# Two reorders: low halves of weights by VectorE outside the first attention; modulation groups under the norms' roots and the first scan keys ahead of x's norm

## The chip, the cores and the metric
One core of one Trainium2 chip runs the whole program. The metric is device microseconds of one execution. A core has five engines that work side by side: TensorE (PE, with its weight loads shown as PEld), VectorE (DVE), ScalarE (ACT), GpSimd (POOL) and SyncE (SP, which here only issues DMAs). Each walks its own instruction list in order and meets the others through semaphores.

## The reference
Two different transformer blocks, each of depth 2, work on 256 tokens of width 1024. Cut to what matters here:

```
def first_block(x, ...):                      # l = 0, 1
    h = rms_norm(x, ln_attn_g[i])             # "a0", "a1"
    ... = split(h @ w_in[i]); y_diff, y_moba = two kinds of causal attention
    x = x + concat([y_diff, y_moba]) @ w_out[i]
    x = x + conv_ffn(rms_norm(x, ln_ffn_g[i]), w_up[i], ..., w_down[i])   # "f0", "f1"

def second_block(x, c, ctx, c_ctx, ...):      # l = 0, 1
    mod_l = silu(c) @ w_ada[l] + b_ada[l]     # shift, scale, gate: 3 x 1024
    mod_c = silu(c_ctx) @ w_ada[l] + b_ada[l]
    h_l = _rmsnorm(x,  g_pre[l]) * (1 + sc_l) + sh_l     # "x0", "x1"
    h_c = _rmsnorm(xc, g_pre[l]) * (1 + sc_c) + sh_c     # "c0", "c1"
    pl, pc = h_l @ w_in[l], h_c @ w_in[l]     # attention, gated linear scan, convolution, gates
    out = (g_a*br_a + g_b*br_b + g_c*br_c) @ w_out[l]
    x = x + gt_l * _rmsnorm(out_l, g_post[l])
```

All arrays are float32.

## The kernel before
**Products.** Each float32 product is made of three matmuls on split numbers: high half by high half, low by high, high by low. Activations and weights are both split. A weight tile of 128 x 1024 (512 KB) is loaded by SyncE (L2552) into one of NR = 5 `RAW` buffers; ScalarE copies its high half to `SPH` (L1335); VectorE (L1873) or GpSimd (L2450) subtracts and writes the low half `SPL`, both into one of NS = 4 slots. TensorE's helper `turned` runs the triples L888 to L890 (weights stationary), `straight` runs L900 to L902 (activations stationary). A `RAW` buffer is free after the low half, a slot after its last matmul.

**One order.** The class `Schedule` is run once to write a single list of steps (loads, splits, products, norms, copies); each engine's program walks that list and emits its own share, so the list fixes the order on every in-order queue, SP's loads among them. `get_w` names the next tile and lets splits run NS + 1 tiles ahead; a load stands in the list NR - 1 tiles ahead of its split. Which engine makes a low half follows a pattern over the split tiles:

```
SPLIT_ON = ((0, 0, 1), (1, 1, 1))
eng = "pool" if self.split_on[self.nsplit % len(self.split_on)] else "dve"
```

The first entry holds outside the first block's attention (every third low half on GpSimd), the second inside it (all on GpSimd, while VectorE does the softmaxes). At the start, and in a few tiles between the two depths of the second block, all are on VectorE; in `group_n` with `by_tile`, the PF = 2 tiles ahead are on GpSimd. The low halves of odd activation tiles of the three branches (`ABL`, L2496) are GpSimd's too.

**The norms.** `norm` adds the step `stats` (VectorE and ScalarE sum the squares, L1935 and L1357, then VectorE takes the root in a chain of small operations L1809 to L1819 and builds diagonal matrices `DG`, L1943) and eight steps `prod`, four matmuls each: TensorE multiplies x by the diagonals (L934), which turns it, and ScalarE and VectorE or GpSimd write the split result `HTH` (L1365, or L1374 and L1377) and `HTL` (L1951, or L2473). For a1, f0, f1 and x0 nothing stands between the last use of the old x and the norm in TensorE's order.

**The modulation.** `ada_te` makes `mod` of depth 0 in six groups of 512 columns of `w_ada`: four steps of eight matmuls straight from `RAW` (L946, no split), a copy of the row by ScalarE (L1341), and eight small matmuls that turn it (L955), then an add on VectorE (L1878). Two groups run in the first attention (`fill`), four in the first feed-forward layer, one step in each of its 24 rounds j:

```
if l == 0:
    next(self.ada, None)
```

After the sixth group VectorE makes `GP`, the scale for c0 and x0 (L1883). c0's products run in the second attention.

**The scan's keys.** After x0's norm come `rank` (24 matmuls with a 32 column weight, L1057 to L1059) and four tiles `gk` of `wgk0`, each 24 matmuls of 512 columns: 256 of context (from c0, ready long before) and 256 of x (from x0). The rest of the second block follows: query projections, the gated linear scan (L2163, L2169, L1111), the branches, attention, gates and the output product.

## Time and profile before

| | before |
|---|---|
| three runs | 2269.45, 2271.2 and 2271.24 us, median 2271.2 |
| the profiled execution's own time | 2270.02 us |
| its span | 2267.9 us |
| TensorE busy, mean granted clock | 2131.5 us (94%), 0.967 |
| VectorE, ScalarE, GpSimd busy | 1326.3, 963.0, 556.8 us |
| low halves on GpSimd, on VectorE | 169, 293 |

The span runs from the first to the last instruction that the profile shows; the execution's own time has another 2.1 us around it. A granted clock of 1 is TensorE's full 2.4 GHz and 0.5 is 1.2 GHz; a mean over a stretch lies between. The text below names the view of each number it uses.

### The profile page before, as it was taken

The page shows a single profiled execution, that of the slowest core. Times are in us where ns is not written, and L with a number is a line of the kernel's source. Part 1 is how long each engine was busy: PE and PEld are TensorE (multiplying, and loading weights), DVE is VectorE, ACT ScalarE, POOL GpSimd, SP SyncE. Part 2 cuts the span into 40 slices and gives each one's busy share as a digit, 9 for nine tenths or more (in the row PEclk, how much of TensorE's full clock was granted, in tenths as well). Part 3 has the DMA queues.
Part 4 walks back from the last instruction along what each step waited for, and adds up shares of the span by engine and source line. Part 5 has one row for each costly group of instructions (what it writes and reads, how often), then busy time and mean ns, then how long its engine had stood idle before and what let it go on. Part 6 is the DMA issues. An engine that isn't in the chain of part 4 may idle for free.

```text
span 2267.9 us, 31387 instructions
## 1 busy us (share of the span) xinstructions
PE 2131.5 (94%) x12074; PEld 1825.8 (81%) x12074; DVE 1326.3 (58%) x2202; ACT 963.0 (42%) x1602; POOL 556.8 (25%) x321
## 2 busy tenths in 40 slices
PE   7888999889899899998999999999999998999998
PEld 5667998667899787887887778888778898888987
DVE  5735666774777513827464453877464577575464
ACT  4434555444455425334332363233343553445443
POOL 1422333152333311111031002222222121321332
PEclk9979999898999999999999999999999999999999
DMA  9434655331455422211132202634224233241543
GB/s 251 132 130 153 242 212 210 127 114 53 146 186 179 154 101 82 67 57 65 57 103 84 75 19 88 226 125 148 95 95 151 93 112 131 89 162 66 172 147 128
DMA packets 79066, 285.00 MB, mean 126 GB/s; under 512 B 8822, under 2 KB 9730, under 8 KB 78920
## 3 DMA queue, kind: packets, MB, share of 16 engines
q1 hardware_dynamic: 70560, 256.15, 33.3%
q10 hardware_dynamic: 6072, 18.73, 2.3%
q0 software_dynamic: 2288, 8.13, 1.4%
q8 instruction: 97, 1.59, 0.3%
q14 instruction: 49, 0.40, 0.1%
HBM read 277.14 MB, written 5.83 MB: 125 GB/s over the span
## 4 chain that ended last, share of the span: by engine, by line
PE 42%; DVE 7%; ACT 3%; issue 2%; POOL 0%; POOLq 0%; DVEq 0%; ACTq 0%
PE pb L888 8%; PE pb L890 8%; PE pb L889 8%; PE pb L900 3%; PE pb L902 3%; PE pb L901 3%; PE pb L1214 2%; PE pb L906 2%; ACT SPH L1335 1%; PE pb L1195 1%; DVE SPL L1873 1%; PE pb L1111 1%; PE pb L1155 1%; DVE GW L2163 1%; DVE ATT L2191 1%
## 5 line engine op out<-in xcount | busy, mean ns | idle before, releaser
L2450 POOL TENSOR_TENSOR SPL<-RAW,SPH 128x1024 fp32r<-128x1024 f32 x169 | 415.8, 2463 | 1058.9 <-ACT SPH L1335 960.1
L1873 DVE TENSOR_TENSOR SPL<-RAW,SPH 128x1024 fp32r<-128x1024 f32 (+1 forms) x293 | 426.5, 1463 | 415.6 <-ACT SPH L1335 386.3
L888 PE MATMUL pb<-HTH,SPH 128*128 128x256 f32 (+1 forms) x1984 | 648.6, 327 | 5.4 <-POOL HTL L2473 2.0
L889 PE MATMUL pb<-HTL,SPH 128*128 128x256 f32 (+1 forms) x1984 | 638.1, 322 | 0.0
L890 PE MATMUL pb<-HTH,SPL 128*128 128x256 f32 (+1 forms) x1984 | 637.8, 321 | 0.0
L1335 ACT ACTIVATE SPH<-RAW 128x1024 fp32r<-128x1024 f32 x462 | 476.5, 1048 | 278.3 <-PE pb L902 117.6
L888 PEld LDWEIGHTS pb<-HTH,SPH 128*128 128x128 f32 x1984 | 382.8, 193 | 39.1 <-issue 6.7
L889 PEld LDWEIGHTS pb<-HTL,SPH 128*128 128x128 f32 x1984 | 383.0, 193 | 27.0
L890 PEld LDWEIGHTS pb<-HTH,SPL 128*128 128x128 f32 x1984 | 382.4, 193 | 27.0
L900 PE MATMUL pb<-SPH,HTH 128*128 128x512 f32 x544 | 221.3, 407 | 19.6 <-DVE SPL L1873 9.0
L901 PE MATMUL pb<-SPH,HTL 128*128 128x512 f32 x544 | 216.4, 398 | 0.0
L902 PE MATMUL pb<-SPL,HTH 128*128 128x512 f32 x544 | 216.3, 398 | 0.0
L900 PEld LDWEIGHTS pb<-SPH,HTH 128*128 128x128 f32 x544 | 105.0, 193 | 47.5 <-issue 11.6
L888 PE MATMUL pb<-ABH,SPH 128*128 128x512 f32 (+1 forms) x384 | 132.0, 344 | 10.4 <-POOL ABL L2496 7.6
L890 PE MATMUL pb<-ABH,SPL 128*128 128x512 f32 (+1 forms) x384 | 130.2, 339 | 0.0
L889 PE MATMUL pb<-ABL,SPH 128*128 128x512 f32 (+1 forms) x384 | 130.1, 339 | 0.0
L902 PEld LDWEIGHTS pb<-SPL,HTH 128*128 128x128 f32 x544 | 104.8, 193 | 23.0
L901 PEld LDWEIGHTS pb<-SPH,HTL 128*128 128x128 f32 x544 | 105.3, 193 | 20.8
L888 PEld LDWEIGHTS pb<-ABH,SPH 128*128 128x128 f32 x384 | 72.5, 189 | 19.5 <-ACT ABH L1746 8.0
L2483 POOL TENSOR_TENSOR AL<-FT,AH 128x256 fp32r<-128x256 f32 x44 | 32.6, 741 | 210.6 <-ACT AH L1466 210.6
L1696 ACT ACTIVATE GT<-pb,BG 128x512 f32<-128x512 f32 (+1 forms) x48 | 27.8, 579 | 127.7 <-PE pb L890 127.7
L890 PEld LDWEIGHTS pb<-ABH,SPL 128*128 128x128 f32 x384 | 72.5, 189 | 8.6
(275 smaller groups left out, 2947.6 us busy)
## 6 DMA issues: line engine op xcount, KB each, us to landing
RAW<-in_w_up SPq DMA_DIRECT2D x88, 512.0 KB, 4.3
RAW<-in_wa SPq DMA_DIRECT2D x64, 512.0 KB, 3.2
RAW<-in_w_in SPq DMA_DIRECT2D x48, 512.0 KB, 4.6
RAW<-in_wmg SPq DMA_DIRECT2D x48, 512.0 KB, 3.3
RAW<-in_wbr SPq DMA_DIRECT2D x48, 512.0 KB, 3.2
RAW<-in_w_down SPq DMA_DIRECT2D x44, 512.0 KB, 3.4
RAW<-in_w_ada SPq DMA_DIRECT2D x24, 512.0 KB, 5.0
ARAW<-in_w_ada ACTq DMA_DIRECT2D x24, 512.0 KB, 4.1
```

The lines of the kernel that those rows point to most:

```text
L888: T.matmul(o, wh[:, kt, :], xh[:, kt, n0:n1], start=kt == 0, stop=False)
L889: T.matmul(o, wh[:, kt, :], xl[:, kt, n0:n1], start=False, stop=False)
L890: m = T.matmul(o, wl[:, kt, :], xh[:, kt, n0:n1], start=False, stop=kt == 7)
L900: T.matmul(P[:, :], xh[:, kt, c], wh[:, j, :], start=kt == 0, stop=False)
L901: T.matmul(P[:, :], xl[:, kt, c], wh[:, j, :], start=False, stop=False)
L902: m = T.matmul(P[:, :], xh[:, kt, c], wl[:, j, :], start=False, stop=kt == 7)
L906: return T.transpose(o, i, ident)
L1214: m = T.matmul(P[:, t * 128:(t + 1) * 128], sb["VV"][:, k0 + i, (h // 4) * 128:(h // 4 + 1) * 128], sb["APT"][:, j % 2, i * 128:(i + 1) * ...
L1335: A.activation(hi, raw, ACT.Copy, scale=1.0).then_inc(*act.tick(s["hi"], ("u", u)))
L1873: W.tensor_tensor(lo, raw, hi.bitcast(F32), SUB).then_inc(*dve.tick(s["lo_dve"], ("u", u)))
L2450: G.tensor_tensor(lo, raw, hi.bitcast(F32), SUB).then_inc(*pool.tick(s["lo_pool"], ("u", u)))
L2483: G.tensor_tensor(sb["AL"][:, i, :], sb["FT"][:, j % 2, :], sb["AH"][:, i, :].bitcast(F32), SUB).then_inc(*pool.tick(s["ffn_pool"], ("al", ...
```

## The change
Three things, in the order list alone and in what follows from it:

- **Low halves.** `SPLIT_ON[0]` becomes `(0,)`: outside the first block's attention every weight's low half is VectorE's. `low_by_pool` names the activation tiles whose low half stays with GpSimd: odd ones of branch a, and of branches b and c at depth 0; at depth 1 those of b and c move to VectorE. In the last group of `w_out`, splits run 6 tiles ahead and not 2.
- **Modulation groups.** A new `norm_filled` puts one group between `stats` and the products of a norm: one under f0 (bank 7), one under a1 (bank 3), one under f1 (bank 7); one stays in the first feed-forward layer, one step in each round j from 1 to 6; two stay in the first attention. `limit` holds back how far splits may run ahead during this. `GP` is made after the fourth group, and `gate_col` waits for the last two.
- **Keys.** The context half (columns 256 to 511) of the first EARLY = 3 key tiles is multiplied ahead of x0's products, which share banks 0 to 6 with the three accumulations that are held; the x half follows the norm, then `rank`, then the fourth tile.

```diff
--- before.py
+++ after.py
@@ -33,12 +33,13 @@
 RA = [2.0, 1.25]
 IC, PC = (4, 5), (8, 15)
 KEYS = ((0,) * 8, (3, 3, 1, 2, 2, 2, 2, 1))
+EARLY = 3
 BO = (4, 4, 4)
 RB = (2, 2, 2.8, 4)
 OUTS = (4, 2, 5)
 RQ = ((.8, .7, 2), (.8, 1, 3))
 GA = [2, 1]
-SPLIT_ON = ((0, 0, 1), (1, 1, 1))
+SPLIT_ON = ((0,), (1,))
 PF = 2
 LT, LV = 2, 3
 
...
@@ -115,6 +116,11 @@
         drain(side)
 
 
+def low_by_pool(l, w, kt):
+
+    return kt % 2 == 1 and (w == "a" or w in "bc" and l == 0)
+
+
 def gla_full(s, l):
 
     return s == 0 or l == 0
...
@@ -189,7 +194,7 @@
         self.gets += 1
         if self.order is not None:
             assert self.order[u] == (name, idx, cols, kind)
-            self.split_upto(u + NS + 1)
+            self.split_upto(min(u + NS + 1, self.limit))
         return u
 
     def put_w(self, u):
...
@@ -213,9 +218,7 @@
                     for u in us:
                         self.put_w(u)
                     if ahead:
-                        self.split_on[:] = (1,)
                         self.split_upto(self.gets - 1 + ahead)
-                        self.split_on[:] = SPLIT_ON[0]
                 yield t
             return
         for i in range(4):
...
@@ -232,6 +235,21 @@
         for _ in self.products(tag, ring):
             next(side, None)
         drain(side)
+
+    def norm_filled(self, tag, ada_ring):
+
+        self.add("stats", tag)
+        self.ada_ring = ada_ring
+        self.limit = self.gets + 4
+        for n, _ in enumerate(self.fill(1)):
+            if n == 4:
+                self.limit += 1
+                self.split_upto(self.limit)
+        for kt, _ in enumerate(self.products(tag, LOW7)):
+            if kt in (1, 4):
+                self.limit += 1
+                self.split_upto(self.limit)
+        self.limit = 1 << 30
 
     def products(self, tag, ring):
         for kt in range(8):
...
@@ -349,7 +367,10 @@
         self.add("bias_back")
 
     def block1(self, l):
-        self.norm(f"a{l}", LOW7, () if l else self.first(), 1)
+        if l:
+            self.norm_filled("a1", (3,))
+        else:
+            self.norm("a0", LOW7, self.first(), 1)
         self.add("lam", l)
         if l:
             self.add("mark", f"qkv{l}")
...
@@ -383,11 +404,12 @@
         drain(first)
         for g in range(2):
             if g:
-                drain(self.group_n(("wo", l, 1), f"w_out{l}", 1, (0, 1), (2, 3), ("Y", l), True))
+                drain(self.group_n(("wo", l, 1), f"w_out{l}", 1, (0, 1), (2, 3), ("Y", l), True, 4 + PF))
             for t in range(2):
                 self.add("res1", l, g, t)
                 self.give(("wo", l, g, t))
-        self.norm(f"f{l}", LOW7)
+        self.norm_filled(f"f{l}", (7,))
+        self.ada_ring = (3,)
         for t in range(2):
             for g in range(2):
                 self.take((4 + 2 * t + g,), ("dn", l, t, g))
...
@@ -401,8 +423,8 @@
                     self.put_w(u)
                 self.add("up", l, j)
                 self.give(n)
-            if l == 0:
-                next(self.ada, None)
+            if l == 0 and 1 <= j < 7:
+                next(self.ada)
             if j == 3 and l == 0:
                 self.add("tables", 0)
             if j == 6 and l == 0:
...
@@ -650,20 +672,35 @@
         if not last:
             self.add("mark", "x1done")
         self.add("wdec", l)
+        early = []
         if not last:
+            self.limit = self.gets + EARLY - 1
+            for ft in range(EARLY):
+                self.take((0, 1, 2, 3), ("gk", l, ft))
+                early.append(self.get_w(f"wgk{l}", ft))
+                self.add("gk_mm", l, ft, early[ft], 1)
             self.norm("x0", LOW7)
             self.add("spill_x")
+            self.limit = 1 << 30
+            self.split_upto(self.gets)
         self.add("mark", f"proj{l}")
+        for ft, u in enumerate(early):
+            self.add("gk_mm", l, ft, u, 0)
+            self.put_w(u)
+            self.split_upto(self.gets + ft + 1)
+            self.add("gk", l, ft)
+            self.give(("gk", l, ft))
         u = self.get_w(f"wr{l}", 0, cols=256)
         n = self.take(ALL8, ("wr", l))
         self.add("rank", l, u, H)
         self.put_w(u)
         self.give(n)
-        for ft in range(4):
+        for ft in range(len(early), 4):
             u = self.get_w(f"wgk{l}", ft)
             n = self.take(ALL8, ("gk", l, ft))
-            self.add("gk", l, ft, u, H)
+            self.add("gk_mm", l, ft, u, None)
             self.put_w(u)
+            self.add("gk", l, ft)
             self.give(n)
         if not last:
             drain(self.gla_queries(0, H))
...
@@ -718,12 +755,10 @@
                     self.give(("w2", l, 0, t))
         if not last:
             self.add("stats", "x1")
-            self.split_on[:] = (0,)
             for t in (2, 3):
                 self.split_upto(self.gets + t - 2)
                 self.x_out(l, t)
             self.split_upto(self.gets + 2)
-            self.split_on[:] = SPLIT_ON[0]
             drain(self.products("x1", LOW6))
             for ft, _ in enumerate(self.gla_queries(1, ("x1",))):
                 if ft == 0:
...
@@ -873,7 +908,7 @@
         if src[0] == "AB":
             _, l, w = src
             pe.wait_ge(s["branch_act"], ("h", l, w, kt))
-            pe.wait_ge(s["branch_pool" if kt % 2 and w != "s" else "branch_dve"], ("l", l, w, kt))
+            pe.wait_ge(s["branch_pool" if low_by_pool(l, w, kt) else "branch_dve"], ("l", l, w, kt))
             return ABH, ABL
         for tag in src:
             pe.wait_ge(s["norm_act"], ("h", tag, kt))
...
@@ -1059,10 +1094,18 @@
             m = T.matmul(P[0:32, :], wl[:, kt, :], xh[:, kt, :], start=False, stop=kt == 7)
         m.then_inc(*pe.tick(mm, ("w", u), ("wr", l)))
 
-    def gk(l, ft, u, src):
-        P = bank(("gk", l, ft))
-        m = turned(P[:, :], *halves(u), src, 0, 512)
-        m.then_inc(*pe.tick(mm, ("w", u), ("gk", l, ft)))
+    def gk_mm(l, ft, u, st):
+
+        src = ("x1", "c1") if l else ("x0", "c0")
+        if st != 0:
+            bank(("gk", l, ft))
+        P = k.P(("gk", l, ft))
+        if st is None:
+            m = turned(P[:, :], *halves(u), src, 0, 512)
+        else:
+            m = turned(P[:, st * 256:st * 256 + 256], *halves(u), src[st:st + 1], st * 256, st * 256 + 256)
+        if not st:
+            m.then_inc(*pe.tick(mm, ("w", u), ("gk", l, ft)))
 
     def gq(l, ft, u, src):
         n = 256 if l else 512
...
@@ -1877,8 +1920,8 @@
         dve.wait_ge(mm, ("ada", g))
         W.tensor_tensor(MT[:, 0, 4 * g:4 * g + 4, :], P[:, 256:264].rearrange("p (j s) -> p j s", j=4),
                         V(par("b_ada", 4 * g, 4), [1, 4], [0, 2]), ADD).then_inc(*dve.free(*k.read(("ada", g))))
-        if g == 5:
-            for i in range(6):
+        if g == 3:
+            for i in range(4):
                 dve.wait_ge(*k.read(("ada", i)))
             W.scalar_tensor_tensor(out=sb["GP"][:, 0, :, :], in0=MT[:, 0, 8:16, :], scalar=1.0,
                                    in1=V(par("g_pre", 0, 8), [1, 8], [0, 2]), op0=ADD, op1=MUL).then_inc(
...
@@ -2354,12 +2397,14 @@
                                op0=MUL, op1=MUL).then_inc(*dve.free(*k.read(("og", l, ft))))
 
     def split_z(l, w, ft):
-        if ft % 2 == 0:
-            split_low(l, w, ft, sb["ZB"][:, 0, 0:256 if l else 512])
+        if not low_by_pool(l, w, ft):
+            split_low(l, w, ft, sb["ZB"][:, ft % 2, 0:256 if l else 512])
 
     def gate_col(l):
         k.past(dve, f"rows{l}")
         dve.wait_ge(s["const_dve"], ("mod", l))
+        for g in () if l else (4, 5):
+            dve.wait_ge(*k.read(("ada", g)))
         for st in range(1 if l else 2):
             W.tensor_tensor(sb["GC"][:, st, :], MT[:, l, 16:24, st], par("g_post", l * 8, 8), MUL).then_inc(
                 *dve.tick(s["branch_dve"], ("gc", l, st)))
...
```

## Rows read from the trace of the kernel before

**Rows 1.** The profile page: engines' busy time, costliest groups, weight loads.
```profile
PE 2131.5 (94%) x12074; PEld 1825.8 (81%) x12074; DVE 1326.3 (58%) x2202; ACT 963.0 (42%) x1602; POOL 556.8 (25%) x321
...
L2450 POOL TENSOR_TENSOR SPL<-RAW,SPH 128x1024 fp32r<-128x1024 f32 x169 | 415.8, 2463 | 1058.9 <-ACT SPH L1335 960.1
L1873 DVE TENSOR_TENSOR SPL<-RAW,SPH 128x1024 fp32r<-128x1024 f32 (+1 forms) x293 | 426.5, 1463 | 415.6 <-ACT SPH L1335 386.3
...
RAW<-in_w_up SPq DMA_DIRECT2D x88, 512.0 KB, 4.3
```

**Rows 2.** Waits of TensorE: releaser, us in total, times, longest.
```profile
PE pb L934 <- DVE DG L1943: 27.2, 5, 7.9
PE pb L1111 <- DVE GW L2169: 11.1, 8, 3.4
...
PE pb L900 <- DVE SPL L1873: 9.0, 5, 3.4
PE pb L888 <- POOL ABL L2496: 7.6, 2, 4.2
```

**Rows 3.** Windows: stretch, length, PE, PEld, DVE, ACT, POOL busy, clock, DMA, GB/s.
```profile
181.65:192.70 11.05, 5.33 (x34) 5.20 (x33) 7.62 (x22) 2.93 (x7) 2.09 (x1) 0.69 0.29 95
...
770.85:785.30 14.45, 6.55 (x34) 6.43 (x33) 6.93 (x20) 6.12 (x13) 3.12 (x5) 0.65 0.26 83
...
1842.00:1912.00 70.00, 60.74 (x476) 59.88 (x475) 58.64 (x78) 25.28 (x33) 12.04 (x5) 0.95 0.34 114
2023.80:2034.00 10.20, 7.04 (x35) 6.23 (x34) 6.46 (x6) 2.10 (x4) 1.76 (x1) 0.67 0.50 183
```

**Rows 4.** Windows, the same columns: the two feed-forward stretches.
```profile
192.70:396.85 204.15, 203.80 (x1483) 183.24 (x1481) 133.16 (x185) 108.44 (x161) 69.29 (x44) 1.00 0.61 217
578.30:770.85 192.55, 189.42 (x1323) 176.27 (x1321) 141.10 (x191) 103.71 (x157) 73.05 (x44) 1.00 0.53 176
```

**Rows 5.** Timeline around norm f0: start, us, engine, operation, idle before.
```profile
182.63 2.19 DVE L1935 SCALAR_TENSOR_TENSOR XN<-XS 128x1024 f32<-128x1024 f32 x1
...
187.53 5.40 PE L934 MATMUL pb<-DG,XS 128*128 128x128 f32 x32 [5.72 <-DVE DG L1943]
```

**Rows 6.** Timeline, TensorE: norm products of a1 and x0, then c1's.
```profile
403.76 6.46 PE L934 MATMUL pb<-DG,XS 128*128 128x128 f32 x32 [6.75 <-DVE DG L1943]
...
778.90 6.62 PE L934 MATMUL pb<-DG,XS 128*128 128x128 f32 x32 [7.90 <-DVE DG L1943]
...
1705.73 0.28 PE L890 MATMUL pb<-HTH,SPL 128*128 128x256 f32 x1
...
1706.81 0.28 PE L890 MATMUL pb<-HTH,SPL 128*128 128x256 f32 x1
1707.10 4.11 PE L934 MATMUL pb<-DG,XS 128*128 128x128 f32 x32
```

**Rows 7.** Timeline, TensorE: one modulation step in the first feed-forward stretch.
```profile
359.05 0.64 PE L946 MATMUL pb<-RAW,CSP 128*32 128x256 f32 x8
```

**Rows 8.** Timeline after x0's norm: rank, a low half of x0, first keys.
```profile
785.27 0.48 PE L1057 MATMUL pb<-HTH,SPH 128*32 128x512 f32 x1
...
787.94 0.74 POOL L2473 TENSOR_TENSOR HTL<-HV,HTH 128x256 fp32r<-128x256 f32 x1 [0.17 <-ACT HTH L1377]
...
789.06 1.22 DVE L1873 TENSOR_TENSOR SPL<-RAW,SPH 128x1024 fp32r<-128x1024 f32 x1 [10.11 <-ACT SPH L1335]
...
790.88 0.39 PE L888 MATMUL pb<-HTH,SPH 128*128 128x512 f32 x1
```

**Rows 9.** Low halves on GpSimd in the second attention: us, busy (count), clock, DMA.
```profile
443.00:550.00 107.00, 34.72 (x15) 0.87 0.27 89
```

**Rows 10.** Timeline of one collision of GpSimd and VectorE, late in the kernel.
```profile
2023.16 2.40 POOL L2450 TENSOR_TENSOR SPL<-RAW,SPH 128x1024 fp32r<-128x1024 f32 x1 [6.51 <-ACT SPH L1335]
...
2023.37 2.73 DVE L2296 TENSOR_TENSOR QNB<-QNB,QT 128x512 f32<-128x512 f32 x1
...
2026.25 0.41 PE L906 MATMUL pb<-IDENT,QNB 128*128 128x128 f32 x2 [1.84 <-DVE QNB L2296]
```

More of the change, by code:

```diff
@@ L132, in __init__ @@
         self.slots, self.raw_before, self.slot_before = [None] * NS, {}, {}
-        self.split_on = [0]
-        self.low_at = {}
+        self.split_on, self.limit = [0], 1 << 30
         self.run()
@@ L1241, in tensor_program @@
             "bias": bias, "qk_turn": qk_turn, "scores": scores, "turn": turn1, "values": values, "y_turn": y_turn,
-            "up_mm": up_mm, "down": down, "rank": rank, "gk": gk, "gq": gq, "gdec": gdec,
+            "up_mm": up_mm, "down": down, "rank": rank, "gk_mm": gk_mm, "gq": gq, "gdec": gdec,
             "gprod": gprod, "gke": gke, "gst": gst, "gout": gout, "ba_mm": ba_mm, "head_turn": head_turn,
@@ L1509, in rank, with gk @@
             *act.free(*k.read(("wr", l))))
-    def gk(l, ft, u, src):
+    def gk(l, ft):
         act.wait_ge(mm, ("gk", l, ft))
@@ L1735, in z @@
             act.wait_ge(s["branch_act"], ("h", l, w, ft - 2))
-            act.wait_ge(s["branch_pool" if ft % 2 else "branch_dve"], ("l", l, w, ft - 2))
+            act.wait_ge(s["branch_pool" if low_by_pool(l, w, ft) else "branch_dve"], ("l", l, w, ft - 2))
         A.activation(sb["ZB"][:, ft % 2, 0:NT], k.P(("z", l, w, ft))[:, 0:NT], ACT.Tanh, scale=0.5).then_inc(
@@ L2504, in split_z @@
     def split_z(l, w, ft):
-        if ft % 2:
+        if low_by_pool(l, w, ft):
             split_low(l, w, ft, sb["ZB"][:, 1, 0:256 if l else 512])
```

## The prediction

> **What bounds the kernel now.** The page first: TensorE is busy 2131.5 of 2267.9 us [rows 1], so at most 136 us of waiting and what a reduced clock costs can be won without taking matmuls away. VectorE is busy 1326 us, GpSimd 557. Then TensorE's waits: the largest entry is the norm's, 27.2 us in five waits on the diagonals `DG` [rows 2]; behind it come waits on VectorE's scan operation L2169, on low halves of weights and, twice, up to 4.2 us, on GpSimd's `ABL`. Then the windows round the norms: in f0's 11.05 us TensorE works 5.33, at a mean granted clock of 0.69; x0's is 14.45 us at 0.65 [rows 3]. The timelines show one shape at f0, a1, f1 (which repeats f0) and x0: TensorE idle for 5.7, 6.75, 5.7 and 7.9 us, then 32 norm products that last 5.40, 6.46 and 6.62 us where c1's, which follow close matmuls, last 4.11 [rows 5, 6]. So TensorE idles, its clock goes towards the 1.2 GHz level, and the next products pay too. Last, pairs of GpSimd and VectorE: a low half of 2.40 us begins at 2023.16, VectorE's L2296 begins 0.21 later and lasts 2.73 us, up to 2026.10, and TensorE waits 1.84 for it [rows 10]. 2.73 is what was left of the 2.40, 2.19, and a remainder of 0.54. The 10 us behind it have clock 0.67 [rows 3].
>
> **Part 1, three modulation groups put under the roots of f0, a1 and f1.** A group in the feed-forward stretch costs its TensorE time. The first such stretch has four groups and the second none: 204.15 against 192.55 us, busy 203.80 against 189.42 [rows 4]: 2.9 us a group by span, 3.6 by busy time. By the operations, four steps of 0.64 [rows 7] and one turn of about 0.9: 3.5. I take 3.4 (bounds 2.9 and 3.6), so 10.2 us leave the two feed-forward and attention paths. In the norm the group costs nothing if it fits the gap. At half clock its steps double to about 1.14 us each, some 5.5 with the turn, and ScalarE's copy of the row adds about 0.8 between them: 6.3 against gaps of 5.7 to 6.75. That is tight, but the first steps run before the clock falls, and the activity itself keeps it up. VectorE's chain of the root has only the small add of the group behind it. The move past SP's queue: the four raw tiles fill four of five `RAW` buffers, so the first `w_up` or `w_in` tiles are issued only when TensorE has finished modulation steps; each lands 3 to 4.3 us later [rows 1], then ScalarE's high half (1.05) and VectorE's low half (1.22 [rows 8]) follow, between the norm's own writes. The 32 products cover 4 to 5 us of this. I book +1.7 for what isn't covered, over three norms (0 to +6). Part 1: -10.2 + 1.7.
>
> **The squares' sum.** At f0 and f1 VectorE's L1935 lasts 2.19 us because a GpSimd low half is running [rows 5]; alone such an operation on 128 x 1024 takes 1.22, by the low half with as many elements [rows 8]. With those low halves on VectorE, behind `stats` in its queue, -0.95 at each: -1.9 (0 to -2).
>
> **Clock in the norms.** With matmuls in the gap the norm's products would last 4.11 and not 5.40 (f0, f1) and 6.46 (a1) [rows 5, 6]: 1.3 + 1.3 + 2.35 = 5.0. The first steps of a group are few columns and may not hold the clock, and ScalarE's and VectorE's copies pace the products: I take a third, -1.6 (0 to -5).
>
> **Part 2, early keys.** A tile's context half is 24 matmuls of 256 columns at 0.12 us (nine pitches from 1705.73 to 1706.81 [rows 6]): 2.88 us, 8.6 for three. They start where TensorE now stops, at 770.9, and end at 779.5, 0.6 after the diagonals are ready at 778.90 [rows 6]. The products then run at the full clock. What ends the norm is the chain behind them: ScalarE takes about 0.95 us per 256 columns of two copies, and the last low half of x0 is done at 788.68 [rows 8]. Before, `rank` covers that; after, the first key tile's x half does, and is done at about 789.05. Then two x halves (5.76), `rank` (785.27 to 790.88: 5.61 [rows 8]), and the fourth tile (5.45): 805.9, against 790.88 + 4 x 5.45 = 812.7. That is -6.8; I take -6.5 (bounds -5, if a weight is late, and -8, if ScalarE starts on the early products' heels).
>
> **Part 3, low halves to VectorE.** GpSimd has 169 low halves of about 2.4 us, of which two times 15, in the attentions, stay (one of these shown [rows 9]): 139 move. Each adds 1.22 us to VectorE alone, and takes GpSimd's reads off it. How often VectorE pays for these now: its 293 own low halves average 1.463 against 1.22 alone, +71 us in this line alone [rows 1, 8], and L1935 and L2296 show that other lines pay too [rows 5, 10]. Added work: 139 x 1.22 = 170. So VectorE's sum rises by something between 0 and 100 us of its 1326, which no one waits for in itself. On TensorE's path I find nine waits that end behind such a pair, 20 us together (the longest 4.2 and, for L2169, 3.4 [rows 2]; 1.84 [rows 10]); of these the collision itself is some 1.4 us each, 12.5. Queueing behind low halves that are now VectorE's gives back 4. The clock behind these waits (10.2 us at 0.67 [rows 3] and three like it) gives back 4, and new waits in dense stretches cost 4. Part 3: -12.5 + 4 - 4 + 4 = -8.5 (bounds +4 and -20).
> The Trainium skill, page "SBUF — State Buffer", section "Who interferes with whom", says that a VectorE instruction with two SBUF inputs contends with a GpSimd instruction that reads SBUF, and that the later one is blocked until the other ends. By that rule, the trace agrees: 2.73 us is the rest of the GpSimd one and most of its own. Taken at its word every moved low half frees VectorE entirely, and part 3 would tend to its -20 end.
>
> **The sum.** -10.2 + 1.7 - 1.9 - 1.6 - 6.5 - 8.5 = -27.0. On the profiled execution's own 2270.0 us (2.1 round its span) that gives 2243.0; the runs' median of 2271.2 stands 1.2 above the profiled one, so 2244.
>
> **The rivals.** (a) VectorE's low halves cost as much as GpSimd's did: part 3 is 0, the rest stands: -18, 2253. For it: VectorE gains net work, and TensorE already waits 9.0 us in five waits on its low halves [rows 2]. Chance 0.20. (b) The norms keep most of their gaps because the tiles behind a modulation group come late: a group hides in TensorE's wait, but 3 us of new wait follow at each of three norms, and part 3 gives half: 2271.2 - 27 + 9 + 4 = 2257. For it: the `RAW` buffers. Against: 3.2 to 4.3 us of landing lie under 5 us of products. Chance 0.08. (c) More: all collision waits and their clock go, and the norms' products run at full clock: 10.2 + 1.9 + 5 + 7 + 12 = 36, 2235. For it the rows of c1. Chance 0.12. (d) Nothing comes of it: the groups in the feed-forward stretch were hidden and the norms' gaps are refilled by waits: 2271. Against: busy 203.80 of 204.15 hides nothing [rows 4]. Chance 0.02. (e) The other side: VectorE's in-order queue becomes the bound. In the scan stretch of depth 1 it is busy 58.64 of 70 us, 84% [rows 3], with 12.04 of GpSimd's beside it. Each moved low half that stands before a scan or softmax operation that TensorE waits for costs 1.2 us there, and gains nothing. Against gains of 18 it decides once more than 15 of the 139 do so, and with 24 the kernel is at 2271 - 18 + 29 = 2282. Against it: most of the 139 lie in stretches where VectorE is busy 65 to 73% [rows 4] and its operation ahead of a low half would have been slowed. Chance 0.03.
> The Trainium skill, page "Perfetto Trace Analysis", section "Optimizing Scalar/DVE Operations", says that work of a saturated DVE may be better on Scalar or GPSIMD, though a shared read port can spoil it. That speaks against this change in the 84% stretch, where it would give (e); the trace bears out the half about the port more than the half about saturation.
>
> **How the numbers follow.** The forecast has 0.55. The bounds of single terms lie far apart (part 3: 24 us), so the range goes from rival (c) with 2 us to spare, 2233, to above (b), 2261; it leaves out (d), (e) and half a tail on either side. A difference under 0.2%, 4.5 us, is about what a measurement of this kernel can't tell from no change. Faster than that: all but (d) and (e) and a remainder, 0.94; same 0.03; slower 0.03.
>
> **What the profile of the changed kernel would show.** Right: TensorE's waits on `DG` fall from 27.2 us to under 8; the first feed-forward stretch is about 8 to 11 us shorter, the second unchanged; x0's keys end 6 to 7 us sooner after the last feed-forward matmul; norm windows have a clock above 0.8; L1873 x432 with a mean near 1.25 us and L2450 x30; waits on `ABL` L2496 at depth 1 gone, L2296 at 0.69 throughout. Wrong: new waits of L888 and L900 on `SPH` or `SPL` directly behind the norm's products (rival b); waits on GW, ATT or QNB that end behind an L1873 (rivals a, e); clock near 0.6 in the norms although TensorE is active.

## The result and the profile after

The changed kernel takes 2211.8 us (median of 4 runs, 2210.3 to 2217.8) against 2270.4 for the kernel before (2269.5 to 2271.2): ratio 0.9747, 95% interval 0.9727 to 0.9766, or some 58 us. The forecast was 2244, with a range down to 2233. The direction was right; the size was not, and the time is below the range.

The profiled execution has a span of 2211.3 us (own time 2213.1) against 2267.9, so 56.6 us have to be found. The page, in the lines that answer to [rows 1]:

```profile
PE 2112.7 (96%) x12146; PEld 1816.3 (82%) x12146; DVE 1361.5 (62%) x2350; ACT 961.3 (43%) x1602; POOL 206.2 (9%) x173
...
L1916 DVE TENSOR_TENSOR SPL<-RAW,SPH 128x1024 fp32r<-128x1024 f32 x433 | 524.2, 1229 | 412.9 <-ACT SPH L1378 397.4
...
L2495 POOL TENSOR_TENSOR SPL<-RAW,SPH 128x1024 fp32r<-128x1024 f32 x29 | 69.3, 2402 | 186.2 <-ACT SPH L1378 137.7
...
RAW<-in_w_up SPq DMA_DIRECT2D x88, 512.0 KB, 4.5
```

TensorE is busy 96% of a shorter span, and for 18.8 us less, although it has 72 more matmuls. Most of that is the clock (mean granted 0.977, before 0.967): it was busy at the 1.2 GHz level for 117.6 us before and is for 84.6 now, and half of the difference, 16.5 us, is what the lower level costs. L1916 is L1873 of before: 433 low halves with a mean of 1.229 us, where 293 had 1.463. So 140 more low halves cost VectorE 524.2 - 426.5 = 98 us in this line, and its whole busy time rose by only 35 us (1326.3 to 1361.5): the rest it got back in other lines. GpSimd's own fell from 169 to 29 (the prediction had 139 moved and 30 left).

TensorE's waits, beside [rows 2] (us in total, times, longest):

```profile
PE pb L935 <- DVE SPL L1916: 6.3, 3, 3.4
PE pb L969 <- DVE DG L1986: 6.2, 4, 2.6
...
PE pb L1154 <- DVE GW L2212: 4.5, 8, 1.4
PE pb L923 <- DVE ABL L2291: 4.3, 2, 2.9
```

The wait for the norms' diagonals went from 27.2 to 6.2 us, GpSimd's `ABL` has left the list of waits at depth 1 (VectorE's `ABL` L2291 has 4.3), L2169's successor L2212 went from 11.1 to 4.5, and the waits on VectorE's low halves, which rival (e) expected to grow, fell from 9.0 in five to 6.3 in three.

The windows that answer to [rows 3]: norm f0, x0's norm with the early keys, the scan of depth 1, and the first 8 us behind the former collision:

```profile
181.95:192.23 10.28, 8.44 (x73) 7.18 (x72) 8.44 (x24) 6.50 (x11) 0.00 (x0) 0.83 0.80 306
745.40:758.60 13.20, 12.69 (x104) 12.26 (x104) 6.53 (x20) 4.86 (x11) 2.17 (x3) 1.00 0.36 124
1806.10:1869.40 63.30, 59.41 (x489) 58.54 (x488) 56.36 (x80) 24.41 (x33) 0.00 (x0) 1.00 0.38 119
1979.50:1987.50 8.00, 6.18 (x45) 5.21 (x43) 4.83 (x7) 2.63 (x6) 0.00 (x0) 1.00 0.74 251
```

Clock 0.83 for 0.69 in f0, 1.00 for 0.65 in x0's norm, 1.00 for 0.95 in the scan and 1.00 for 0.67 behind the collision. The scan's window is a little wider than that of before: the same matmuls took 70.1 us before and take 61.8 now. The two feed-forward stretches, beside [rows 4]:

```profile
192.23:384.20 191.97, 191.97 (x1361) 178.01 (x1360) 133.59 (x202) 102.75 (x156) 16.35 (x22) 1.00 0.57 196
557.42:745.30 187.88, 187.87 (x1321) 176.33 (x1321) 136.98 (x213) 103.72 (x157) 16.45 (x22) 1.00 0.54 178
```

The first went from 204.15 to 191.97 us, the second from 192.55 to 187.88, although no modulation group was ever in it.

To see where the 56.6 us arise, the same matmul was looked up in both traces, and the difference of its start times taken. Plotted over time it is a stair: flat where both kernels are equally fast, a step where one gains. Its treads were read at these places (times of before):

| up to | stretch | this stretch gives |
|---|---|---|
| 187.5 | start, first attention, wait of f0 | -0.7 |
| 394.0 | f0's products, first feed-forward layer | -11.9 |
| 411.2 | norm a1 | -0.8 |
| 447.5 | projections of the second attention | -6.6 |
| 573.1 | second attention, wait of f1 | -1.0 |
| 768.0 | second feed-forward layer | -4.3 |
| 807.2 | x0's norm and keys | -6.8 |
| 1233.0 | scan of depth 0 | -5.0 |
| 1844.3 | branches to output, depth 0 | +1.2 |
| end | depth 1 of the second block | -20.7 |

The first feed-forward layer and x0's norm with its keys account for 18.7 of it. The other 38 lie elsewhere, over half of them in the last fifth of the kernel, which only the low halves touch. Single treads are good to a few us only: the start differs by 1 to 3 us between executions, and two steps of +1.2 and +1.5 us behind 1270 and 1630 stand in this trace and in e2's, but not in e4's or e5's.

The f0 norm after, on TensorE, beside [rows 5]:

```profile
182.01 1.93 PE L981 MATMUL pb<-RAW,CSP 128*32 128x256 f32 x32
184.44 1.05 PE L990 MATMUL pb<-SEL,AROW 128*128 128x2 f32 x8 [0.50 <-ACT AROW L1384]
186.84 5.44 PE L969 MATMUL pb<-DG,XS 128*128 128x128 f32 x32 [1.34 <-DVE DG L1986]
192.23 0.39 PE L923 MATMUL pb<-HTH,SPH 128*128 128x256 f32 x1
```

The 32 modulation matmuls and the 8 that turn the row are in what was an idle gap of 5.72 us, with 0.5 us of waiting for ScalarE's copy between them; the norm's products start at 186.84, earlier than the 187.53 of before, and the first product of the feed-forward layer follows them at once. The group takes 3.5 us here, up to 185.49, where the prediction had 6.3. So the group is free. The norm's products are no faster: 5.44 us against 5.40.

x0's norm after, on TensorE, beside [rows 6, 8]:

```profile
745.46 0.28 PE L923 MATMUL pb<-HTH,SPH 128*128 128x256 f32 x1
...
754.08 2.88 PE L969 MATMUL pb<-DG,XS 128*128 128x128 f32 x24
757.28 0.71 PE L969 MATMUL pb<-DG,XS 128*128 128x128 f32 x4 [0.32 <-ACT HV L1417]
758.18 0.71 PE L969 MATMUL pb<-DG,XS 128*128 128x128 f32 x4 [0.19 <-ACT HV L1417]
...
760.56 0.36 PE L923 MATMUL pb<-HTH,SPH 128*128 128x256 f32 x1 [0.24 <-ACT HTH L1420]
...
769.59 0.39 PE L1092 MATMUL pb<-HTH,SPH 128*32 128x512 f32 x1
```

Early products from 745.46 to 754.1, then x0's; from 757.28 on each group of four waits for ScalarE's `HV`, and the first key's x half waits 0.2 to 0.4 us four times on ScalarE's and GpSimd's halves: the chain behind the products sets the pace, as in the prediction.

The former collision of [rows 10], in the changed kernel:

```profile
1978.00 0.69 DVE L2339 TENSOR_TENSOR QNB<-QNB,QT 128x512 f32<-128x512 f32 x1
...
1978.61 1.22 DVE L1916 TENSOR_TENSOR SPL<-RAW,SPH 128x1024 fp32r<-128x1024 f32 x1
...
1980.17 0.82 PE L941 MATMUL pb<-IDENT,QNB 128*128 128x128 f32 x6
1982.81 0.39 PE L923 MATMUL pb<-HTH,SPH 128*128 128x256 f32 x1 [1.82 <-DVE S L2354]
```

L2339 is L2296 of before. It takes 0.69 us instead of 2.73, a low half on VectorE stands right behind it, and TensorE comes to its turn at 1980.17 without a wait. The price comes next: TensorE waits 1.82 us for VectorE's `S`, which stands behind two more low halves; before, it waited for `S` twice there, 0.97 and 0.35 us. In sum the same matmuls, up to 2034.1 of before, take 5.9 us and not 10.2.

### The profile page after: what moved, and what is told of

Read it like the earlier page. It is cut to its first block, busy times and chain, and to the rows that moved or that the text cites. A ratio compares the mean times of both kernels' runs of the same rounds, so it can differ in the third digit from the quotient of the medians.

```text
span 2211.3 us, 31532 instructions
## 1 busy us (share of the span) xinstructions
PE 2112.7 (96%) x12146; PEld 1816.3 (82%) x12146; DVE 1361.5 (62%) x2350; ACT 961.3 (43%) x1602; POOL 206.2 (9%) x173
## 4 chain that ended last, share of the span: by engine, by line
PE 69%; DVE 8%; ACT 4%; issue 2%; POOL 0%; DVEq 0%; ACTq 0%
PE pb L923 13%; PE pb L925 13%; PE pb L924 13%; PE pb L935 5%; PE pb L937 5%; PE pb L936 5%; PE pb L941 2%; PE pb L1154 2%; PE pb L1257 2%; PE pb L1238 1%; DVE SPL L1916 1%; ACT SPH L1378 1%; PE pb L1082 1%; PE pb L1081 1%; PE pb L1080 1%
## 5 line engine op out<-in xcount | busy, mean ns | idle before, releaser
L1916 DVE TENSOR_TENSOR SPL<-RAW,SPH 128x1024 fp32r<-128x1024 f32 x433 | 524.2, 1229 | 412.9 <-ACT SPH L1378 397.4
L2495 POOL TENSOR_TENSOR SPL<-RAW,SPH 128x1024 fp32r<-128x1024 f32 x29 | 69.3, 2402 | 186.2 <-ACT SPH L1378 137.7
L924 PEld LDWEIGHTS pb<-ABL,SPH 128*128 128x128 f32 x384 | 72.3, 188 | 8.5 <-issue 0.2
```

What stands on the lines that cost most here:

```text
L924: T.matmul(o, wh[:, kt, :], xl[:, kt, n0:n1], start=False, stop=False)
L1916: W.tensor_tensor(lo, raw, hi.bitcast(F32), SUB).then_inc(*dve.tick(s["lo_dve"], ("u", u)))
L2495: G.tensor_tensor(lo, raw, hi.bitcast(F32), SUB).then_inc(*pool.tick(s["lo_pool"], ("u", u)))
```

## The experiments

Theory A: the mechanism of part 3 was right and its size was wrong; what the collisions cost was taken too small, and the costs set against it too large. Theory B: the terms were right one by one, and the parts help each other. Theory C: it isn't VectorE being held up that costs, but that a low half by GpSimd is ready later.

**Each part alone, on the kernel before** (e1 to e3), and part 3 in depth 1 of the second block alone (e4).

e1, low halves:
```
-SPLIT_ON = ((0, 0, 1), (1, 1, 1))
+SPLIT_ON = ((0,), (1,))
...
+def low_by_pool(l, w, kt):
+    return kt % 2 == 1 and (w == "a" or w in "bc" and l == 0)
```
The 6 tiles ahead in the last group of `w_out` are not in this run; they went with e2.

> The kernel before with part 3 alone (every weight's low half outside the first block's attention, and the odd activation tiles of branches b and c at depth 1, on VectorE). Theory A (collisions were under-sized): the gain in the stretches without a norm, measured from the two traces as about 38 us of the 56.6, is this part's alone: 2232 +- 4. Theory B (the sum of the prediction was right term by term and the parts help each other): about 2260 +- 4, and the missing 30 us show only where all three are together.

Measured: 2230.8 us, ratio 0.9825 (0.981 to 0.984): about -40 us, as theory A said. Its page:

```profile
PE 2119.7 (95%) x12074; PEld 1818.3 (82%) x12074; DVE 1364.9 (61%) x2350; ACT 964.4 (43%) x1602; POOL 205.1 (9%) x173
...
L1909 DVE TENSOR_TENSOR SPL<-RAW,SPH 128x1024 fp32r<-128x1024 f32 x433 | 526.7, 1232 | 424.8 <-ACT SPH L1371 409.9
```

The same 12074 matmuls, in the same order, are busy 11.8 us less (2131.5 to 2119.7); the span is 37.7 shorter, so 26 us are waits. Of these only 2.4 are the norms':

```profile
PE pb L962 <- DVE DG L1979: 24.8, 5, 7.2
```

The stair against the kernel before (its times) steps where the pairs were: -4.5 between 411 and 435, -2.0 at 768, -4.9 between 1879 and 1911, -1.0 at 1974, -4.8 between 2026 and 2034, -3.6 between 2107 and 2116, -2.5 between 2183 and 2196. Each has a jump at the wait, and most have a ramp beside it, in which the clock of before was low. Nine waits stand at these seven places, 19.5 us together before; I take them for the nine of the prediction.

Since the matmuls of e1 and of before can be paired one by one, the 37.7 us can be split by what TensorE did before each of them, and set beside the terms of part 3:

| | prediction | e1 |
|---|---|---|
| the nine waits | -12.5 | -14.3 |
| other waits that got shorter | 0 | -13.2 |
| norm waits (booked under the squares' sum) | | -2.4 |
| waits that got longer | +8 | +4.0 |
| busy time by the clock | -4 | -9.1 |
| busy time at the full clock | 0 | -2.7 |

The clock's share is half of what TensorE was busy at the 1.2 GHz level, 117.6 us before and 99.3 in e1. One of the other waits, before and in e1:

```profile
1089.15 2.40 POOL L2450 TENSOR_TENSOR SPL<-RAW,SPH 128x1024 fp32r<-128x1024 f32 x1 [14.91 <-ACT SPH L1335]
1089.14 2.69 DVE L2219 SCALAR_TENSOR_TENSOR WA<-WA,PAR 128x255 f32<-128x255 f32 x1
...
1096.40 0.79 PE L1111 MATMUL pb<-GW 128*128 128x128 f32 x5 [2.65 <-DVE GW L2169]
```

```profile
1081.28 1.91 PE L1147 MATMUL pb<-GW 128*128 128x128 f32 x15 [0.38 <-DVE GW L2205]
```

VectorE's L2219 takes 2.69 us beside a GpSimd low half and 0.48 in e1; three operations later in VectorE's queue come the ones on `GW`, and TensorE's wait for them goes from 2.65 us to 0.38. That each of the other waits stood behind such a pair was not looked up.

e2, modulation groups:
```
-        self.norm(f"f{l}", LOW7)
+        self.norm_filled(f"f{l}", (7,))
+        self.ada_ring = (3,)
...
-            if l == 0:
-                next(self.ada, None)
+            if l == 0 and 1 <= j < 7:
+                next(self.ada)
```


> The kernel before with the modulation groups alone moved under f0, a1 and f1. Theory A: the first feed-forward stretch shorter by 11.9 us, the norms no shorter, so 2258 +- 3. Theory B: less than 8 us alone (2262 or more), because the tiles behind each norm are still late by a GpSimd low half.

Measured: 2257.5 us, ratio 0.9945 (0.9928 to 0.9963): about -13. Its first feed-forward stretch and its wait for the diagonals:

```profile
191.27:386.70 195.43, 195.09 (x1360) 178.63 (x1360) 132.34 (x180) 102.66 (x156) 67.61 (x44) 1.00 0.56 192
```

```profile
PE pb L970 <- DVE DG L1987: 14.4, 5, 7.9
```

195.43 against 204.15: 2.9 us a group, the lower bound of the prediction. The remaining 27.2 - 14.4 = 12.8 us of norm waits are where the groups now run. Beyond the 8.7 us the stair has -0.6 to -1.7 at the norms, and -4.8 between 408 and 436: there two waits on low halves, 0.65 and 2.17 us before, are gone. My reading is that GpSimd's low halves no longer meet VectorE's work there, because the splits stand elsewhere in the order. Between 1233 and 1844 the stair gives 3.1 back, nearly all of it the two steps that differ between executions.

e3, early keys:
```
+            for ft in range(EARLY):
+                self.take((0, 1, 2, 3), ("gk", l, ft))
+                early.append(self.get_w(f"wgk{l}", ft))
+                self.add("gk_mm", l, ft, early[ft], 1)
             self.norm("x0", LOW7)
```


> The kernel before with the early keys alone. Theory A: -6.8 us as between the traces, 2263.5 +- 2. Theory B: under 4 us alone, 2266.5 or more.

Measured: 2264.9 us, ratio 0.9973 (0.9964 to 0.9983): -6.0. The longest wait on the diagonals, x0's 7.9 us, is gone:

```profile
PE pb L969 <- DVE DG L1986: 19.0, 4, 6.8
```

The three alone give -40.1, -13.4 and -6.0, together -59.5, against 58.6 measured for all. In sum they add up, and theory B, which needed 30 us from parts helping each other, falls. Stretch by stretch they add up less well: the first feed-forward layer with f0's products gives 12 us with all parts and 8.8 and under 1 with the first two alone, while the 6.6 us behind a1 come whole from the low halves and 4.5 of them also from the groups. These two differences, of some 3 and 4 us, go opposite ways.

e4, part 3 for the last depth only (42 weight tiles and 8 activation tiles):
```
         last = l == 1
+        if last:
+            self.split_on[:] = (0,)
```


> The kernel before with part 3 only in the last depth of the second block (some 35 weight tiles and 8 activation tiles; the rest as before). Between the traces this depth gained 20.7 us. Theory A: the gain stands by itself, 2250 +- 3. Theory B: under 8 us, 2262 or more.

Measured: 2249.9 us, ratio 0.9907 (0.9892 to 0.9922): -21 us, by itself. Its page shows part of a repair:

```profile
L1916 DVE TENSOR_TENSOR SPL<-RAW,SPH 128x1024 fp32r<-128x1024 f32 x335 | 467.4, 1403 | 420.7 <-ACT SPH L1378 398.7
...
L2493 POOL TENSOR_TENSOR SPL<-RAW,SPH 128x1024 fp32r<-128x1024 f32 x127 | 312.5, 2464 | 738.6 <-ACT SPH L1378 646.2
```

335 low halves on VectorE with a mean of 1.403 us, between before and after.

**Is it the collision?** In the changed kernel, where VectorE makes all these low halves, GpSimd was given work that nobody waits for:
```
     def split(u):
         raw, hi, lo, eng = k.slot(u)
+        if u in sched.ghosts:                      # every third tile, depth 1, from the keys on
+            k.past(pool, "kv1")
+            pool.wait_ge(s["hi"], ("u", u))
+            if s["ghost"].n:
+                pool.wait_ge(s["ghost"], s["ghost"].n)
+            G.tensor_tensor(GHOST, IDENT8, IDENT8, SUB)...      # e5: reads SBUF, 128x1024
+            for _ in range(3): G.memset(GHOST, 0.0)...          # e6 instead: reads nothing
```


> The changed kernel, with 27 extra subtractions of 128 x 1024 on GpSimd in the last stretch of the kernel (from the keys and values of depth 1 on, one for every third weight tile, when its high half is ready, as GpSimd's low halves stood before). They read the identity matrix in SBUF and write a scratch tile that nothing reads; VectorE still makes every low half. No one waits for them except GpSimd's own queue. Between the traces the stretch behind 1909 us of before gained 14.2 us. Theory A (what costs is the hold-up of VectorE while GpSimd reads SBUF): most of it comes back, +7 to +14 us on 2211.8, and lines of VectorE again show operations longer by up to 2.4 us. Theory C (what cost was that a low half of GpSimd is ready later, 2.4 us and not 1.2): 0 to +2 us, since every low half is as early as in the changed kernel.

Measured: 2233.8 us (2233.1 to 2236.3): +22 us on 2211.8, where theory A expected 7 to 14. The 27 operations take 1.9 us each. On the stair the last stretch, from 1860 us of the changed kernel on, costs 24 us, 17.4 of them waits of TensorE.

```profile
L1920 DVE TENSOR_TENSOR SPL<-RAW,SPH 128x1024 fp32r<-128x1024 f32 x433 | 560.8, 1314 | 397.1 <-ACT SPH L1382 384.2
```

```profile
PE pb L927 <- DVE ABL L2295: 9.1, 2, 4.9
...
PE pb L927 <- DVE SPL L1920: 6.0, 7, 1.2
```

```profile
2066.61 1.90 POOL L2498 TENSOR_TENSOR GHOST<-IDENT 128x1024 f32<-128x1024 f32 x1 [10.36 <-ACT SPH L1382]
2066.62 2.96 DVE L1920 TENSOR_TENSOR SPL<-RAW,SPH 128x1024 fp32r<-128x1024 f32 x1 [0.58 <-ACT SPH L1382]
```

The low half and the extra operation wait for the same high half, start 0.01 us apart, and VectorE's takes 2.96 us, which is the 1.90 of GpSimd's and 1.06. Behind it in VectorE's queue stand two operations on `ZB` and, behind ScalarE's half, `ABL`; TensorE's L927 waits 4.16 us for it at 2071.43, and in the changed kernel the same wait was 1.40. The mean of the low halves goes from 1.229 up to 1.314. Theory C has nothing to say to this, since the low halves are in the same places and on the same engine. It is weak for the kernel before too: of TensorE's waits there only two, 0.6 us together, end on a weight's low half from GpSimd.

The run shows that such a hold-up costs, and not how much of e1's 40 us it was. It is harder than before: each extra operation waits for the same high half as VectorE's low half, and 21 of the 27 stretch one to 2.9 us or more, where GpSimd's low halves met whatever VectorE was doing.

> As the run before, but each of the 27 is three fills of the scratch tile (128 x 1024, no input): GpSimd is occupied at the same places and reads no SBUF. Theory A: 0 to +2 us, VectorE's operations keep their lengths. If instead an occupied GpSimd is what costs (its own sums and low halves of activations queue behind), as much as the run before.

Measured: 2215.7 us (2214.4 to 2216.7), +3.9 on 2211.8, a little more than expected, though GpSimd was occupied longer (81 fills of 0.956 us, 77 us in all, against 51). VectorE's low halves kept their length:

```profile
L1920 DVE TENSOR_TENSOR SPL<-RAW,SPH 128x1024 fp32r<-128x1024 f32 x433 | 524.1, 1229 | 411.5 <-ACT SPH L1382 403.7
```

The 3.9 lie in the same last stretch, which costs 4.5 us on the stair, 2.5 of them waits. There nine operations of VectorE got longer, by 4.8 us together, each beside a fill, and all nine are TENSOR_SCALAR:

```profile
1923.17 2.98 POOL L2498 MEMSET GHOST<- 128x1024 f32 x3 [6.64 <-ACT SPH L1382]
1924.19 0.98 DVE L1858 TENSOR_SCALAR RS<-RS 128x8 int32<-128x8 int32 x1
```

In the changed kernel this operation takes 0.17 us:

```profile
1926.57 0.17 DVE L1854 TENSOR_SCALAR RS<-RS 128x8 int32<-128x8 int32 x1
```

It and the one ahead of it (0.99 for 0.17) stand before TensorE's wait for `S` at 1928.5, and that wait is 2.11 us and not 0.49: the 1.62 are the two hold-ups. So a GpSimd that only writes let VectorE's subtractions pass and held up some TENSOR_SCALAR operations, for 4 us; a GpSimd that reads SBUF beside VectorE costs 22 us.

e7, only the 8 activation tiles on VectorE:
```
-    return kt % 2 == 1 and w != "s"
+    return kt % 2 == 1 and (w == "a" or w in "bc" and l == 0)
```


> The kernel before, with only the 8 odd activation tiles of branches b and c at depth 1 on VectorE. TensorE waited 7.6 us in two waits for such tiles on GpSimd. Theory A: the tile itself (0.73 us) is not what was late but VectorE's work ahead of it, held up by a GpSimd low half of a weight: at most 3 us, 2268 or more. Theory C: most of the 7.6 us and their clock, 2262 or less.

Measured: 2269.5 us, ratio 0.9991 (0.9981 to 1.0): -1.4 us, and 4 at most by the interval. TensorE's waits named GpSimd's `ABL` as releaser for 7.6 us. With the tiles on VectorE the two waits are 3.08 and 3.83 us for 3.42 and 4.19, which is the tile's own difference (0.74 us on GpSimd, 0.43 on VectorE); with the weights' low halves moved too (e1) they are 1.40 and 2.89. So what was late stood ahead of the tile. The name in the list of waits is the last link and not the cause. Theory C would have had most of the 7.6 here.

**How far does it go?** The rest asked whether VectorE's queue has a limit, rival (e), and whether a better version is near.

e8 and e11, low halves of the first block's attention on VectorE: `SPLIT_ON = ((0,), (0,))`, and `((0,), (1, 0))` for every second.

> The changed kernel with the first block's attention's low halves on VectorE too (29 more). Theory A without a limit: a further gain like the 0.29 us a tile of the rest, -8 us, 2204. The rival (e) of the prediction (VectorE's queue becomes the bound where it is busiest): the softmaxes on VectorE are what TensorE waits for there, each low half adds up to 1.2 us: up to +20 us; I expect +3 to +15.

> The changed kernel with every second low half of the first block's attention on VectorE, the rest on GpSimd. With all on VectorE the time was within 3 us of the changed kernel. Theory A: between: 2209 to 2214, no clear difference.

Measured: 2214.2 us (2208.1 to 2218.9) and 2216.3 (2212.3 to 2216.7). Neither is clearly different from 2211.8 (2210.3 to 2217.8). For e8 neither the further gain of 8 us came nor the loss of 3 to 15; e11 lies 2 us above the range that was expected. In e8 the waits show a trade:

```profile
PE pb L935 <- ACT QKT L1448: 7.3, 3, 3.3
...
PE pb L941 <- DVE E L2077: 6.1, 4, 2.6
...
PE pb L1049 <- ACT PT L1468: 3.7, 6, 0.8
```

The softmax's `E` (3.6 in three waits in the changed kernel) and `QKT` (6.1) are waited for longer, 3.7 us in sum; ScalarE's `PT` for 4.8 us less (8.5 before). There VectorE seems to gain from fewer collisions about what it pays in its queue.

e9, all activation tiles on VectorE (`low_by_pool` gives `False`), and e12, that and the 32 sums of the branches:
```
+        if bi:
+            dve.wait_ge(*k.read(name))
+            ...
+            W.tensor_tensor(S, S, g, ADD).then_inc(*dve.tick(s["branch_pool"], ("s", l, bi, ft)))
```


> The changed kernel with the last 20 low halves of activation tiles on VectorE too (odd tiles of branch a at both depths, and of b and c at depth 0). GpSimd takes 0.73 us or more for one, VectorE 0.42 to 0.7. Theory A: small collisions remain with them, but few stand before a wait of TensorE: -4 to +2 us on 2211.8. Rival (e), that VectorE is at its limit: slower by 2 us or more.

> The changed kernel with the last 20 low halves of activation tiles and the 32 sums of the gated branches (128 x 512 or 128 x 256, until now GpSimd's, which read SBUF twice) on VectorE: GpSimd then reads SBUF beside VectorE only in the first block and in norms. Theory A: VectorE's operations around the branches lose their last lengthening (a sum on GpSimd lasts 0.7 to 1.7 us), at the price of 32 x about 0.5 us of its own: -6 to 0 us on 2211.8. Rival (e) (VectorE's queue at its limit in the last stretches): +2 us or more.

Measured: 2212.3 us (2210.2 to 2214.2) and 2212.7 (2211.1 to 2215.8). No change, where e9 allowed -4 to +2 and e12 -6 to 0: what still collides stands before no wait that matters.

e10, `EARLY = 4`:

> The changed kernel with all four key tiles' context halves ahead of x0's products. With three, the early products end 0.6 us or so after the diagonals are ready, so the fourth (2.88 us) delays x0's products by 2.9 us; what ends the norm is ScalarE's chain behind them, which starts as much later. It moves the half of the fourth tile, 2.88 us, to no empty place: +-1 us of 2211.8, and up to +2 since three banks are left for the eight products and not four.

Measured: 2214.6 us (2213.9 to 2215.5), perhaps 3 us slower (expected up to 2) and inside the spread of the changed kernel's own runs. No version that beats the changed kernel was found.

## Why the prediction was wrong, step by step

- **Modulation groups.** Forecast -10.2, and with the clock and the late splits -10.1; alone -13.4. A group is worth 2.9 us (the bound by span; I took 3.4), three are 8.7. It fits the gap with more room than said: 3.5 us at f0 for 6.3. The clock in the norms' products gave nothing at f0 (5.44 for 5.40 us) and 0.5 at a1 (5.94 for 6.46), less than the 1.6 booked. The late splits cost nothing that can be seen. (I took 4.3 us as the longest landing of a weight tile; for `w_in` the page has a median of 4.6.) What came unforeseen are some 4.8 us behind a1, which I read as two colliding pairs that the moved order parts. That reading is from the trace of one run and was not tested by itself.
- **Early keys.** Forecast -6.5; -6.8 between the traces and -6.0 alone. The pace was ScalarE's, as worked out.
- **Squares' sum.** L1978 at f0 takes 1.23 us and no longer 2.19, and TensorE's wait at f0 and at f1 in e1 is 4.99 for 5.73: -0.7 at each for the expected -0.95. x0's wait, for which I booked nothing, gave 0.75 too.
- **Low halves: the step that failed.** "Of these the collision itself is some 1.4 us each, 12.5. Queueing [...] gives back 4. The clock behind these waits [...] gives back 4, and new waits in dense stretches cost 4", in sum -8.5. Measured alone: -40.1, of which about 2 are the squares' sums. The mechanism was right: e5, where GpSimd reads beside VectorE, costs 22 us, and e6, where it only writes, 4. The size was wrong by 30 us, and the table under e1 says where. The nine waits were priced nearly right (12.5 booked, 14.3 measured), though single ones fell by more than a collision's length (3.43 us to 0.49 for `GW` at 1907.7). What failed are the other terms. First, all other waits stood at nothing, and gave 13.2 us: I had priced only waits that I had paired with a collision by eye, and left out such as the 2.65 at 1096.4. Second, the clock stood at 4 and gave 9.1. The row that I took it from says more: 10.2 us at 0.67 are up to 3.4 us lost (an estimate, 10.2 x 0.33, and an upper bound, since TensorE waits in part of it), so four such stretches are up to some 13. Third, 8 us were set against it for queueing and new waits, for which neither a row nor a count stood; the waits that grew are 4.0, of which 1.7 at a softmax's `PT` and 1.1 at `S` behind the former collision. The last 2.7 are busy time that got shorter at the full clock; no run says why.
- **Signs.** Three of the signs of being right did not come: the first feed-forward stretch is 12.2 us shorter and not 8 to 11, the second, called unchanged, 4.7 shorter. And a1's norm has a clock of 0.73, not above 0.8 (0.62 before).
- **The rule of the skill.** By the Trainium skill, page "SBUF — State Buffer", section "Who interferes with whom", the later of two such instructions is blocked until the other ends. I noted that taken at its word it would put part 3 at its -20 end, and left my value at -8.5. In e5 the trace agrees with the rule (2.96 us is 1.90 and 1.06), and even its end of the range was half of what the kernel gained.
- **Rivals.** (e), VectorE's queue as the bound, did not come in the stretch where I had placed it: the same matmuls there fell from 70.1 us to 61.8, with VectorE busy 89% of the window and not 84%. It shows only in small, in the waits that grew. (a) had part 3 at nothing and falls with e1. (b) falls with the norms' waits, 6.2 us, and with products that follow the norm at once. (c), more than forecast, was the direction, with 36 us where 58 came: it had 12 us for the collision waits and their clock, where e1 has 27.5 and 9.1.

## What to carry to other kernels

Where two engines hold each other up, don't price the repair by the waits that you can pair with a collision by eye: here these held 14 of 38 us. As much again lay in other waits, and 9 us in the clock behind them, though the lengthening itself stood on the page (VectorE's low halves averaged 1.463 us against 1.22). Price the clock from the rows of the stretches behind the waits: length times the missing share is its upper bound. Don't set a round cost against a gain either: 8 us were set here where 4 came. A name in the list of waits (here `ABL` on GpSimd, 7.6 us) is the last link: moving that tile alone brought 1.4 us.

## What the runs showed of the hardware

- A GpSimd subtraction of 128 x 1024 from one matrix of 128 x 128 read eight times takes 1.90 us, where one that reads two full tiles takes 2.40.
- A VectorE subtraction that starts 0.01 us after it takes 2.96 us and not 1.22. Its own part behind the release, 1.06, is a little shorter than the whole operation alone; no run shows why.
- 81 fills by GpSimd of 0.956 us each left the mean of VectorE's 433 low halves at 1.229 us; 27 reading operations of 1.90 raised it to 1.314.
- The fills are not harmless for every operation of VectorE: a TENSOR_SCALAR on 128 x 8 that takes 0.17 us took 0.98 and 0.99 beside a fill. Nine operations got longer by over 0.1 us, all TENSOR_SCALAR, none of the subtractions.
- The granted clock in the norm f0 rose from 0.69 to 0.83 with 40 matmuls in the gap, yet the norm's own 32 products took as long (5.44 and 5.40 us); at x0, after 72 products of 256 columns without a pause, the first 24 took 2.88 us, which is the full clock.
